# Layer norms finished on VectorE, X itself turned, the modulation row fetched ahead of them

## The chip, the core and the metric

The kernel runs on one core of a Trainium2 chip. The metric is device time in microseconds of one execution. The core has TensorE (matrix products and turnings, in the rows PE, its weight loads PEld), VectorE (DVE), ScalarE (ACT), GpSimd (POOL) and SyncE (SP), which issues most DMAs. Each engine runs its own list of instructions in order and waits on semaphores that others raise.

## The reference

256 rows of 1024 numbers pass through a post-norm block of two layers and then a block with modulation. Per layer of the first block:

```python
x = layer_norm(ALPHA * x + y, ln_g[i, 0], ln_b[i, 0])        # y: mLSTM mixer, or pooling mixer
x = layer_norm(ALPHA * x + memory_cross_attn(x, ...), ln_g[i, 1], ln_b[i, 1])
x = layer_norm(ALPHA * x + sq_relu_mlp(x, ...), ln_g[i, 2], ln_b[i, 2])
# layer_norm: (x - mean) * rsqrt(var + eps) * g + b
# sq_relu_mlp: square(relu(x @ w1 + b1)) @ w2 + b2
```

The second block takes six vectors from `c`: `silu(c) @ w_ada + b_ada` (the modulation row), normalizes by root mean square, scales and shifts by them, and runs a mixer of two kinds of attention and a SwiGLU; the reference's last step is a norm with `g_final`.

## The kernel before

All arithmetic is in float32 made of two parts: for every product the operand is split into a high part (type fp32r) and a low part (the rest), and three products are summed: high by high, low weight by high, high weight by low. ScalarE makes the high part of each 1 MB piece of weights (`hi_to`, L971), VectorE the low part (`lo_to`, L1504), in rings of four pieces (`raw`, `wh`, `wl`). SyncE refills a `raw` place as soon as its low part is made. So VectorE's list sets when pieces arrive.

`X` and `U` hold the 256 rows as two tiles of 128 (`t` = 0, 1) by 1024 columns, in halves `h` of 512. `XH`, `XL` hold the same turned, columns on partitions, high and low. A layer norm (`layer_norm`, `turn_norm`, `ln_head`) goes: VectorE adds the sublayer's output to ALPHA times X (L1718), takes statistics (L1721 to L1725); GpSimd makes the inverse root (L2133); VectorE writes z = (u - mean) * r into U (L1735); TensorE turns U (`ln_turn`, L413); ScalarE and VectorE apply g and b, now one number per partition, while they empty the bank (L1118, L1677), and make high and low parts (L1123, L1681, L1686). GpSimd makes X itself out of U later, row by row, with g and b copied to all partitions (`bv`; L2166, L2168), and before an MLP it multiplies X by ALPHA and adds the bias b2 (L2175, L2177). Two norms, at the end of each layer (`layer_norm_rows`), write X on VectorE (L1750, L1757).

`pair` is the first product behind a norm: two weight pieces by the rows of t = 0, then of t = 1, while VectorE is still busy with t = 1. In the cross-attention (`xattn`) four heads go through scores (L601), softmax, turning (L611), ScalarE's copy of the turned weights (`turned`, L1169), and the product with the values (L620). In the MLP (`mlp`), 16 steps j: `up(j)` (L329 to L336), ScalarE's relu (L1212), its square as high part (L1220), the same square in float32 on VectorE (L1817), the low part from it (L1821, tile `FLT`), and `down(j)` (L348 to L357). Twelve steps of each MLP also bring in 1 MB of `w_ada`, which VectorE adds into `MOD` (L1493). `MOD` starts as zeros (L2189) with b_ada in its first row (L2190, semaphore `d_mod`); both are on GpSimd's list, behind the first two norms of the first layer.

## Time and profile before

| | us |
|---|---|
| three timed runs | 1053.34 (median), 1053.26, 1059.33 |
| profiled execution, its own time | 1058.63 |
| its span, first to last instruction | 1056.8 |
| TensorE busy / its weight loads | 992.2 / 894.7 |
| VectorE / ScalarE / GpSimd busy | 711.5 / 494.1 / 148.8 |
| mean granted TensorE clock | 0.975 |

The profiled execution took 1.83 us more than its span. Its own time is 5.29 us over the median; of the timed runs two lie by 1053.3 and one by 1059.3.

### The profile page before, as it was taken

The numbers are of one execution on the slowest core, as the hardware profiler recorded it, in microseconds if no ns is written. First come the engines' busy times: TensorE is split into PE (matmuls) and PEld (weight loads), VectorE is DVE, ScalarE is ACT, GpSimd is POOL, SyncE is SP. The second block draws the span as 40 slices with busy tenths as digits, with TensorE's granted clock in tenths as the row PEclk, the third lists the DMA queues.
The fourth block names the chain that finished last, engine by engine and source line by source line (L and its number), as shares of the span: only waits on it lengthen the run. The fifth ranks groups of instructions, "written<-read, shape, count | busy, mean of one in ns | idle before, by whom it ended". The sixth has DMA issues, their size and how long they took to land.

```text
span 1056.8 us, 15072 instructions
## 1 busy us (share of the span) xinstructions
PE 992.2 (94%) x6249; PEld 894.7 (85%) x6249; DVE 711.5 (67%) x815; ACT 494.1 (47%) x674; POOL 148.8 (14%) x122
## 2 busy tenths in 40 slices
PE   6999999899399999989997999999999899999997
PEld 6877988888298998888886998997989689999996
DVE  4874568856687776798599867746786775544453
ACT  4665365436144444354363444443766574334341
POOL 0000111605700001125057000000400000000000
PEclk9999999999699999999998999999999999999999
DMA  8773362723588787627337987852654238565521
GB/s 281 249 239 120 120 223 96 239 87 113 181 309 283 260 292 243 206 80 239 94 114 244 339 296 256 299 157 84 188 178 145 95 104 267 167 200 167 192 80 40
DMA packets 114527, 200.03 MB, mean 189 GB/s; under 512 B 5122, under 2 KB 85368, under 8 KB 111388
## 3 DMA queue, kind: packets, MB, share of 16 engines
q1 hardware_dynamic: 111340, 188.38, 53.4%
q0 software_dynamic: 2832, 10.16, 2.7%
q8 instruction: 50, 0.82, 0.3%
q10 hardware_dynamic: 288, 0.52, 0.1%
q14 instruction: 17, 0.14, 0.0%
HBM read 198.00 MB, written 1.05 MB: 188 GB/s over the span
## 4 chain that ended last, share of the span: by engine, by line
PE 72%; DVE 14%; ACT 5%; issue 4%; POOL 3%; DMA 2%; SPq 1%; DVEq 0%; POOLq 0%; ACTq 0%
PE YB L357 11%; PE YB L348 11%; PE YB L353 10%; PE WB L329 10%; PE WB L336 10%; PE WB L332 10%; DVE wl L1504 6%; PE WB L353 2%; PE WB L348 2%; PE WB L357 2%; ACT wh L971 2%; PE WB L620 2%; DMA raw<-in_mlstm_w_in 1%; DVE BN L1721 1%; DVE U L1718 1%
## 5 line engine op out<-in xcount | busy, mean ns | idle before, releaser
L1504 DVE TENSOR_TENSOR wl<-raw,wh 128x2048 fp32r<-128x2048 f32 (+2 forms) x153 | 370.0, 2427 | 137.4 <-ACT wh L971 136.8
L971 ACT CAST wh<-raw 128x2048 fp32r<-128x2048 f32 (+2 forms) x153 | 288.9, 1892 | 58.9 <-PE YB L357 26.3
L329 PE MATMUL WB<-XH,wh 128*128 128x256 f32 x1024 | 146.7, 285 | 1.3 <-ACT XH L1044 1.3
L332 PE MATMUL WB<-XH,wl 128*128 128x256 f32 x1024 | 144.0, 283 | 0.0
L336 PE MATMUL WB<-XL,wh 128*128 128x256 f32 x1024 | 143.7, 283 | 0.0
L357 PE MATMUL YB<-wh,FLT 128*128 128x512 f32 x360 | 115.9, 404 | 26.3 <-DVE FLT L1821 26.3
L329 PEld LDWEIGHTS WB<-XH,wh 128*128 128x128 f32 x1024 | 135.3, 192 | 6.0 <-ACT AR L1022 1.7
L332 PEld LDWEIGHTS WB<-XH,wl 128*128 128x128 f32 x1024 | 132.4, 192 | 0.0
L336 PEld LDWEIGHTS WB<-XL,wh 128*128 128x128 f32 x1024 | 132.1, 192 | 0.0
L348 PE MATMUL YB<-wh,FHT 128*128 128x512 f32 x360 | 115.9, 404 | 0.0
L353 PE MATMUL YB<-wl,FHT 128*128 128x512 f32 x360 | 114.2, 399 | 0.0
L357 PEld LDWEIGHTS YB<-wh,FLT 128*128 128x128 f32 x360 | 69.2, 193 | 42.9 <-DVE FLT L1821 27.2
L353 PEld LDWEIGHTS YB<-wl,FHT 128*128 128x128 f32 x360 | 69.2, 192 | 16.7
L348 PE MATMUL YB<-wh,XH 128*128 128x256 f32 (+3 forms) x336 | 76.2, 339 | 4.0 <-ACT XH L1123 3.5
L348 PEld LDWEIGHTS YB<-wh,FHT 128*128 128x128 f32 x360 | 66.9, 194 | 12.9
L357 PE MATMUL YB<-wh,XL 128*128 128x256 f32 (+3 forms) x336 | 71.7, 330 | 1.0 <-DVE XL L1841 0.8
L353 PE MATMUL YB<-wl,XH 128*128 128x256 f32 (+3 forms) x336 | 72.0, 331 | 0.0
L1493 DVE SCALAR_TENSOR_TENSOR AR<-raw,SM,AR 128x2048 f32<-128x2048 f32 x24 | 58.6, 2441 | 15.9 <-DMA AR<-in_b_ada 15.2
L348 PEld LDWEIGHTS YB<-wh,XH 128*128 128x128 f32 x336 | 53.1, 192 | 10.5 <-ACT XH L1123 5.0
L357 PEld LDWEIGHTS YB<-wh,XL 128*128 128x128 f32 x336 | 52.9, 191 | 6.8 <-DVE XL L1841 1.0
L353 PEld LDWEIGHTS YB<-wl,XH 128*128 128x128 f32 x336 | 52.8, 191 | 5.2
L2133 POOL TENSOR_TENSOR BN<-BN,SM 128x1 f32<-128x1 f32 x18 | 10.7, 593 | 304.3 <-DVE BN L1725 303.8
(314 smaller groups left out, 1081.7 us busy)
## 6 DMA issues: line engine op xcount, KB each, us to landing
raw<-in_mlp_w SPq DMA_DIRECT2D x64, 1024.0 KB, 5.6
raw<-in_w_ada SPq DMA_DIRECT2D x24, 1024.0 KB, 5.7
raw<-in_mlstm_w_in SPq DMA_DIRECT2D x12, 1024.0 KB, 7.4
raw<-in_w_ffn_gate SPq DMA_DIRECT2D x11, 1024.0 KB, 5.3
raw<-in_w_ffn_up SPq DMA_DIRECT2D x11, 1024.0 KB, 5.4
raw<-in_w_ffn_down SPq DMA_DIRECT2D x11, 1024.0 KB, 4.9
raw<-in_mem_w_kv SPq DMA_DIRECT2D x8, 1024.0 KB, 5.4
raw<-in_xattn_wq SPq DMA_DIRECT2D x8, 1024.0 KB, 6.1
```

The source lines that it names most:

```text
L329: e.matmul(o, H[:, at(k)], xh[:, k, :], start=k == 0, stop=False)
L332: e.matmul(o, L[:, at(k)], xh[:, k, :], start=False, stop=False)
L336: f = e.matmul(o, H[:, at(k)], xl[:, k, :], start=False, stop=k == a - 1)
L348: e.matmul(o, xh[:, k0 + k, tk], pick(H, k), start=start and k == 0, stop=False)
L353: e.matmul(o, xh[:, k0 + k, tk], pick(L, k), start=False, stop=False)
L357: f = e.matmul(o, xl[:, k0 + k, tk], pick(H, k), start=False, stop=stop and k == a - 1)
L620: p = e.matmul(W[:, 256 * d:256 * d + 256], VM[:, m, 256 * h + 128 * d:256 * h + 128 * d + 128], PT[:, 256 * m:256 * m + 256], start=m == ...
L971: f = e.copy(w[:, 0:a * b], raw[:, 0:a * b])
L1493: e.scalar_tensor_tensor(acc, raw[:, :], CACT[:, k:k + 1], acc, ALU.mult, ALU.add).then_inc(w_ada.add(n))
L1504: f = e.tensor_tensor(L[:, 0:a * b], raw[:, 0:a * b], H[:, 0:a * b].bitcast(F32), ALU.subtract)
L1718: e.scalar_tensor_tensor(U[:, t, cs], X[:, t, cs], alpha, YB[2 * t + h][:, :], ALU.mult, ALU.add).then_inc(dve_ln.add(("u", s, t, h)))
L2133: e.tensor_tensor(o, x, MH[:, 0:o.shape[1]], ALU.pow).then_inc(sem_)
```

## The change

- Every layer norm is now one class, `Norm`. `head` is as before; `centre` writes (u - mean) * g into U, `scale` writes that times r plus b into X, both on VectorE and by halves. TensorE turns X, four blocks in one bank; ScalarE casts a half to XH with one copy, VectorE takes the low part from the bank (`low`). GpSimd no longer updates X. The norms of the second block keep U.
- b2 / ALPHA is added to X on VectorE in steps 4 to 7 of an MLP, and ALPHA stays in `head`.
- In the MLP ScalarE squares into float32 and then copies to the high part; VectorE's own square is gone.
- The zeros of MOD and the b_ada row come ahead of the first norm on GpSimd's list.
- In `pair`, low parts of weights by high parts of rows come before the high weights by low parts, and the turning of t = 1 is split in halves between the products. Behind the amid place of `rows` only half of t = 0 is turned there, the other half after the last product.
- In `xattn` ScalarE casts one more piece of weights ahead of the first softmax, and the first copy of turned weights comes ahead of the second softmax. In the mLSTM the first two heads come ahead of the first keys piece.
- In the norm behind the pooling mixer, low parts of the mixer come between the two halves of `head`, and one low part of weights ahead of the second tile.

```diff
+                def first(n, t):
+
+                    hi = ln_hi(s, t) if n == 0 else None
+                    e.wait_ge(*w_hi[ms[n]])
+                    part(n, t, WH, XH, range(4), hi, start=True)
+                    e.wait_ge(*w_lo[ms[n]])
+                    part(n, t, WL, XH, range(4))
+                    part(n, t, WH, XH, range(4, 8), hi)
+                    part(n, t, WL, XH, range(4, 8))
+
+                for n in range(2):
+                    e.wait_ge(*free(n))
+                    first(n, 0)
+                part(0, 0, WH, XL, range(8), ln_lo(s, 0), stop=True)
+                ln_turn(s, 1, 0)
+                part(1, 0, WH, XL, range(8), stop=True)
+                ln_turn(s, 1, 1)
+                for n in range(2):
+                    first(n, 1)
+                    key = ("pair",) + names[n]
+                    part(n, 1, WH, XL, range(8), ln_lo(s, 1) if n == 0 else None, stop=True).then_inc(cnt.add(key))
+                    ends[ms[n]] = cnt[key]
...
+            def by_row(s):
+
+                return s not in ("mix", "ffn")
+
+            def ln_turn(s, t, h):
+
+                if by_row(s):
+                    e.wait_ge(*dve_ln["x", s, t, h])
+                    turn(("ln", s, t, h), lambda k: X[:, t, 128 * k:128 * k + 128], range(4 * h, 4 * h + 4), pe_turn)
...
+                s = f"{i}{j}"
+                for t in range(2):
+                    for h in range(2):
+                        W = bank_of.get(("ln", s, t, h), WB[0])
+                        e.wait_ge(*pe_turn["ln", s, t, h])
+                        e.copy(XH[:, 4 * h:4 * h + 4, 128 * t:128 * t + 128],
+                               W[:, :].rearrange("p (k c) -> p k c", k=4)).then_inc(act_ln.add(("hi", s, t, h)))
+                    if t == 0:
+                        hi_to(m)
...
                 q(2)
+                hi_to(M["wq", i, 3] + 3)
                 scores(0)
                 q(3)
+                turned(0)
                 scores(1)
...
-                    W, R = bank_of.get(("w1", i, j), WB[0]), R0[:, 512 * (j % 2):512 * (j % 2) + 512]
+                    W, R = bank_of.get(("w1", i, j), WB[0]), R0[:, 0:512]
+                    RS = R0[:, 512 + 512 * (j % 2):1024 + 512 * (j % 2)]
...
+                        e.wait_ge(*dve_mlp["h", i, j - 2])
+                    e.activation(RS, R, ACT.Square).then_inc(act_mlp.add(("s", i, j)))
+                    if j > 1:
                         hi_to(M["w2", i, j - 2] + 3)
                         e.wait_ge(*ends.get(M["w2", i, j - 2], (act_own, 1)))
-                    e.activation(FH[j % 2], R, ACT.Square).then_inc(act_mlp.add(("h", i, j)))
+                    e.wait_ge(*act_mlp["s", i, j])
+                    e.copy(FH[j % 2], RS).then_inc(act_mlp.add(("h", i, j)))
...
+                def centre(self, t, h):
+                    s, cs = self.s, slice(512 * h, 512 * h + 512)
+                    e.wait_ge(*self.g_in)
+                    e.scalar_tensor_tensor(U[:, t, cs], U[:, t, cs], BN[:, t, 12:13], BV[self.g][:, cs],
+                                           ALU.subtract, ALU.mult).then_inc(dve_ln.add(("c", s, t, h)))
+
+                def scale(self, t, h):
+                    s, cs = self.s, slice(512 * h, 512 * h + 512)
+                    e.wait_ge(*self.b_in)
                     e.wait_ge(*po_ln["r", s, t])
-                    e.tensor_scalar(U[:, t, cs], U[:, t, cs], BN[:, t, 12:13], BN[:, t, 14:15], ALU.subtract, ALU.mult
-                                    ).then_inc(dve_ln.add(("z", s, t, h)))
-
...
+                    e.wait_ge(*dve_ln["c", s, t, h])
+                    e.scalar_tensor_tensor(X[:, t, cs], U[:, t, cs], BN[:, t, 14:15], BV[self.b][:, cs],
+                                           ALU.mult, ALU.add).then_inc(dve_ln.add(("x", s, t, h)))
+
+                def low(self, t, h):
+                    s = self.s
+                    W, at_ = bank_of.get(("ln", s, t, h), WB[0]), (slice(None), slice(4 * h, 4 * h + 4),
+                                                                  slice(128 * t, 128 * t + 128))
+                    e.wait_ge(*act_ln["hi", s, t, h])
+                    e.tensor_tensor(XL[at_], W[:, :].rearrange("p (k c) -> p k c", k=4), XH[at_].bitcast(F32),
+                                    ALU.subtract).then_inc(dve_ln.add(("lo", s, t, h)))
+                    freed["ln", s, t, h] = dve_ln["lo", s, t, h]
+
+                def first(self):
+
                     for h in range(2):
...
+                        self.centre(0, h)
+                        self.scale(0, h)
+
+                def second(self):
+
+                    self.head(1, 0)
+                    self.head(1, 1)
+                    self.centre(1, 0)
+                    self.low(0, 0)
+                    self.scale(1, 0)
+                    self.low(0, 1)
+                    self.centre(1, 1)
+                    self.scale(1, 1)
+                    self.low(1, 0)
+                    self.low(1, 1)
...
-                    step(e.tensor_tensor(RS, R, R, ALU.mult))
                     if j > 1:
                         lo_to(M["w2", i, j - 2] + 3)
+                    RS = R0[:, 512 + 512 * (j % 2):1024 + 512 * (j % 2)]
                     e.wait_ge(*act_mlp["h", i, j])
                     e.tensor_tensor(FL[j % 2], RS, FH[j % 2].bitcast(F32), ALU.subtract
                                     ).then_inc(dve_mlp.add(("h", i, j)))
+                    if 4 <= j < 8:
+                        n, b_in = bv_of.get(("b2", i), (0, (d_bv[0], 16)))
+                        t, h = divmod(j - 4, 2)
+                        cs = slice(512 * h, 512 * h + 512)
+                        e.wait_ge(*b_in)
+                        e.scalar_tensor_tensor(X[:, t, cs], BV[n][:, cs], 1 / ALPHA, X[:, t, cs], ALU.mult, ALU.add
+                                               ).then_inc(dve_mlp.add(("b2", i, t, h)))
...
+            n10 = Norm(1, 0, "pool", lambda t, h: dve_ln["x", "02", t, h])
+            n10.head(0, 0)
+            pool_lows(1)
+            n10.head(0, 1)
+            n10.first()
+            lo_to(M["pool",] + 2)
+            n10.second()
             lo_to(M["pool",] + 3)
...
-                e.wait_ge(*dve_ln["lo", s, 1, 3])
-                for t in range(2):
-                    e.wait_ge(*g_in)
-                    step(e.tensor_tensor(X[:, t, :], U[:, t, :], BV[gi][:, :], ALU.mult))
-                    e.wait_ge(*b_in)
-                    e.tensor_tensor(X[:, t, :], X[:, t, :], BV[bi][:, :], ALU.add).then_inc(po_x.add((s, t)))
-                users[:] = [po_x[s, 1]] * 2
+                users[:] = [dve_ln["x", s, 1, 1]] * 2
 
             def before_mlp(i):
-                n, b_in = bvec(("b2", i), I["mlp_b2"][i])
-                e.wait_ge(*po_x[f"{i}1", 1])
-                for t in range(2):
-                    step(e.tensor_scalar(X[:, t, :], X[:, t, :], ALPHA, None, ALU.mult))
-                    e.wait_ge(*b_in)
-                    e.tensor_tensor(X[:, t, :], X[:, t, :], BV[n][:, :], ALU.add).then_inc(po_x.add((f"mlp{i}", t)))
-                users[n] = po_x[f"mlp{i}", 1]
+                n, _ = bvec(("b2", i), I["mlp_b2"][i])
+                users[n] = dve_mlp["b2", i, 1, 1]
...
             e.wait_ge(*pe_mlstm["c", 3, 1])
+            step(e.memset(MOD, 0.0))
+            e.dma_start(MOD[0:1, :], I["b_ada_2"][0].rearrange("(a c) -> a c", a=1)).then_inc(d_mod, 16)
             layer_norm(0, 0)
             layer_norm(0, 1)
-            step(e.memset(MOD, 0.0))
-            e.dma_start(MOD[0:1, :], I["b_ada_2"][0].rearrange("(a c) -> a c", a=1)).then_inc(d_mod, 16)
             e.dma_start(WM, I["c_win"]).then_inc(d_wm, 16)
```

GpSimd's list from the second norm's X updates (before) and from the last mLSTM head (changed) on:

```order
L2166 TENSOR_TENSOR X<-U,bv 128x1024
L2168 TENSOR_TENSOR X<-X,bv 128x1024
L2189 MEMSET AR 128x6144
L2190 DMA AR<-in_b_ada 1x16x384
L2191 DMA AR<-in_c_win 128x1088
L2128 DMA bv<-in_mlp_b 128x1024
L2175 TENSOR_SCALAR X<-X 128x1024
```

```order
L2229 TENSOR_TENSOR SM<-SM 128x1
L2257 MEMSET AR 128x6144
L2258 DMA AR<-in_b_ada 1x16x384
L2209 DMA bv<-in_ln_g 128x1024
L2209 DMA bv<-in_ln_b 128x1024
L2214 TENSOR_TENSOR BN<-BN,SM 128x1 x2
```

The zeros and the b_ada row stood behind the X updates; now they stand ahead of the first norm's g and b, and no X update is left.

VectorE's list from the second tile of the norm ahead of the first MLP up to the MLP's first low part (L1821, now L1889):

```order
L1735 TENSOR_SCALAR U<-U,BN 128x512 x2
L1677 TENSOR_SCALAR S<-WB,PC 128x128 x2
L1681 CAST XH<-S 128x2x128
L1677 TENSOR_SCALAR S<-WB,PC 128x128 x2
L1681 CAST XH<-S 128x2x128
L1686 TENSOR_TENSOR XL<-S,XH 128x2x128 x4
L1504 TENSOR_TENSOR wl<-raw,wh 128x2048 x2
L1493 SCALAR_TENSOR_TENSOR AR<-raw,SM,AR 128x2048
L1504 TENSOR_TENSOR wl<-raw,wh 128x2048
L1817 TENSOR_TENSOR AR<-AR 128x512
L1821 TENSOR_TENSOR FLT<-AR,FHT 128x512
```

```order
L1790 SCALAR_TENSOR_TENSOR U<-U,BN,bv 128x512
L1806 TENSOR_TENSOR XL<-WB,XH 128x4x128
L1798 SCALAR_TENSOR_TENSOR X<-U,BN,bv 128x512
L1806 TENSOR_TENSOR XL<-WB,XH 128x4x128
L1790 SCALAR_TENSOR_TENSOR U<-U,BN,bv 128x512
L1798 SCALAR_TENSOR_TENSOR X<-U,BN,bv 128x512
L1806 TENSOR_TENSOR XL<-WB,XH 128x4x128 x2
L1559 TENSOR_TENSOR wl<-raw,wh 128x2048 x2
L1548 SCALAR_TENSOR_TENSOR AR<-raw,SM,AR 128x2048
L1559 TENSOR_TENSOR wl<-raw,wh 128x2048
L1889 TENSOR_TENSOR FLT<-AR,FHT 128x512
```

The copies out of the bank and VectorE's square went; centre, scale and low part alternate. Two pieces of weights, the w_ada piece (L1493, now L1548) and one more piece still stand ahead of the first low part of the MLP.

ScalarE's list in the cross-attention; L1159 (now L1210) is the exponential, L1169 (now L1220) the copy of turned weights:

```order
L971 CAST wh<-raw 128x2048
L1150 COPY AR<-WB 128x512 x2
L1159 ACTIVATE AR,SM<-WB,SM 128x256 x2
L971 CAST wh<-raw 128x2048
L1150 COPY AR<-WB 128x512
L1159 ACTIVATE AR,SM<-WB,SM 128x256 x2
L1169 COPY AR<-WB 128x512
```

```order
L1016 CAST wh<-raw 128x2048
L1201 COPY AR<-WB 128x512 x2
L1016 CAST wh<-raw 128x2048
L1210 ACTIVATE AR,SM<-WB,SM 128x256 x2
L1201 COPY AR<-WB 128x512
L1220 COPY AR<-WB 128x512
L1210 ACTIVATE AR,SM<-WB,SM 128x256 x4
```

The cast of weights went ahead of the first exponential, and the copy ahead of the second.

## Rows read from the trace of the kernel before

**Rows 1.** The page's first part: busy time of TensorE, share of the span.

```profile
PE 992.2 (94%) x6249; PEld 894.7 (85%) x6249; DVE 711.5 (67%) x815; ACT 494.1 (47%) x674; POOL 148.8 (14%) x122
```

**Rows 2.** TensorE's waits: line, who ended them; us in total, times, longest.

```profile
PE YB L357 <- DVE FLT L1821: 26.3, 2, 18.3
...
PE WB L620 <- ACT AR L1169: 5.3, 2, 2.7
...
PE YB L348 <- ACT XH L1123: 3.5, 6, 0.6
```

**Rows 3.** Busy time by stretch, with granted clock, DMA share and rate.

```profile
core 0: us, PE busy (x) PEld busy (x) DVE busy (x) ACT busy (x) POOL busy (x), PEclk, DMA share, GB/s
...
260.00:285.00 25.00, 6.68 (x36) 5.58 (x35) 11.68 (x6) 4.82 (x7) 22.86 (x11) 0.63 0.46 164
...
335.00:430.00 95.00, 95.00 (x614) 86.56 (x614) 67.17 (x41) 43.57 (x42) 6.27 (x4) 1.00 0.79 265
```

**Rows 4.** Timeline of TensorE, 263 to 288 us (start, length, instructions, idle before).

```profile
263.14 0.62 PE L353 MATMUL YB<-wl,FHT 128*128 128x512 f32 x2
...
282.08 1.22 PE L357 MATMUL YB<-wh,FLT 128*128 128x512 f32 x2 [18.32 <-DVE FLT L1821]
...
287.31 0.63 PE L357 MATMUL YB<-wh,FLT 128*128 128x512 f32 x2
```

**Rows 5.** Timeline of VectorE over the same stretch.

```profile
251.43 6.71 DVE L1504 TENSOR_TENSOR wl<-raw,wh 128x2048 fp32r<-128x2048 f32 x2
...
273.29 2.35 DVE L1493 SCALAR_TENSOR_TENSOR AR<-raw,SM,AR 128x2048 f32<-128x2048 f32 x1 [15.15 <-DMA AR<-in_b_ada]
...
280.62 1.41 DVE L1821 TENSOR_TENSOR FLT<-AR,FHT 128x512 fp32r<-128x512 f32 x1
```

**Rows 6.** Timeline of GpSimd over the same stretch.

```profile
251.59 4.39 POOL L2166 TENSOR_TENSOR X<-U,bv 128x1024 f32<-128x1024 f32 x1 [5.72 <-DVE XL L1686]
...
265.15 5.22 POOL L2189 MEMSET AR<- 128x6144 f32 x1
...
270.66 0.60 POOL L2190 DMA_DIRECT2D AR<-in_b_ada  x1 [0.29 <-POOL AR L2189]
```

**Rows 7.** Timeline of VectorE at the second MLP's start.

```profile
548.00 4.50 DVE L1493 SCALAR_TENSOR_TENSOR AR<-raw,SM,AR 128x2048 f32<-128x2048 f32 x1
```

**Rows 8.** Timeline of TensorE at the second MLP's start.

```profile
561.68 1.22 PE L357 MATMUL YB<-wh,FLT 128*128 128x512 f32 x2 [7.97 <-DVE FLT L1821]
...
566.97 0.69 PE L357 MATMUL YB<-wh,FLT 128*128 128x512 f32 x2
```

**Rows 9.** Timeline of VectorE in front of the first cross-attention.

```profile
182.62 15.51 DVE L1504 TENSOR_TENSOR wl<-raw,wh 128x2048 fp32r<-128x2048 f32 x4
```

**Rows 10.** Timeline of TensorE in the first cross-attention.

```profile
208.07 3.12 PE L620 MATMUL WB<-AR,KV 128*128 128x256 f32 x8 [2.67 <-ACT AR L1169]
...
213.72 1.89 PE L620 MATMUL WB<-AR,KV 128*128 128x256 f32 x8
...
215.80 0.71 PE L348 MATMUL YB<-wh,XH 128*128 128x512 f32 x2
```

**Rows 11.** VectorE groups by form (busy us, mean ns | idle before): z, shifted rows.

```profile
L1735 DVE TENSOR_SCALAR U<-U,BN 128x512 f32<-128x512 f32 x16 | 8.0, 544 | 2.4 <-POOL BN L2133 2.0
...
L1757 DVE SCALAR_TENSOR_TENSOR X<-U,BN,bv 128x512 f32<-128x512 f32 x8 | 5.7, 748 | 0.1
```

**Rows 12.** Timeline of TensorE, mLSTM output and third normalization turned.

```profile
150.83 0.62 PE L357 MATMUL YB<-wh,FLT 128*128 128x512 f32 x2
...
460.80 1.04 PE L413 MATMUL WB<-IDN,U 128*128 128x128 f32 x8
```

**Rows 13.** Timeline of VectorE at the same two places.

```profile
144.93 2.15 DVE L1658 SCALAR_TENSOR_TENSOR FLT<-WB,PC,FHT 128x128 fp32r<-128x128 f32 x8
...
465.78 2.29 DVE L1504 TENSOR_TENSOR wl<-raw,wh 128x2048 fp32r<-128x2048 f32 x1
```

**Rows 14.** DMA issues: KB each, median us from issue to landing.

```profile
bv<-in_ln_b POOLq DMA_DIRECT2D x6, 512.0 KB, 5.0
```

More of the change, by code:

```diff
@@ L387, in pair, with part @@
                 ms = [M[n] for n in names]
-                for t in range(2):
-                    for n, m in enumerate(ms):
-                        if t == 0:
-                            e.wait_ge(*free(n))
-                        f = tm(m, 8, 256, 0, 256, YB[n][:, 256 * t:256 * t + 256], t, 0, True, True,
-                               hi=ln_hi(s, t) if n == 0 else None, lo=ln_lo(s, t) if n == 0 else None,
-                               amid=(lambda: ln_turn(s, 1)) if t == 0 and n == 1 else None)
-                        if t == 1:
-                            f.then_inc(cnt.add(("pair",) + names[n]))
-                            ends[m] = cnt[("pair",) + names[n]]
+                def part(n, t, w, x, ks, wait=None, start=False, stop=False):
+                    for k in ks:
+                        if wait:
+                            wait(k)
+                        f = e.matmul(YB[n][:, 256 * t:256 * t + 256], x[:, k, 128 * t:128 * t + 128],
+                                     w[ms[n] % NS][:, 256 * k:256 * k + 256], start=start and k == 0,
+                                     stop=stop and k == 7)
+                    return f
+                def first(n, t):
[18 more added lines that the diff above has]
+                    ends[ms[n]] = cnt[key]
             def turn_pair(key, src, ready, cnt):
@@ L651, in xattn @@
                 values(3)
-                rows(s_, 2, [("wo", i, 2), ("wo", i, 3)], [x(2), x(3)], False, True, amid=lambda: ln_turn(after, 0))
+                rows(s_, 2, [("wo", i, 2), ("wo", i, 3)], [x(2), x(3)], False, True, amid=lambda: ln_turn(after, 0, 0))
+                ln_turn(after, 0, 1)
             def mlp(i, s, late=None):
@@ L1765, in xattn, with layer_norm @@
+            def layer_norm(i, j, rows, x_in):
+                n = Norm(i, j, rows, x_in)
+                n.head(0, 0)
+                n.head(0, 1)
+                n.first()
+                n.second()
             def xattn(i):
@@ L1877, in vector @@
             mlp(1, KV, late)
-            head, centre, scale = layer_norm_rows(1, "w21", lambda t: po_x["mlp1", t])
+            n12 = Norm(1, 2, "w21", lambda t, h: dve_mlp["b2", 1, t, h])
             def rms_z(s, t, h):
```

210 lines of the change are left out of this document (93 added, 117 removed).

## The prediction

> **What bounds the kernel now.** I read the page's busy times first: TensorE is at work in 94% of the span [rows 1], so only its remaining idle time and time at the lower clock can be won. In 95 us of an MLP in full flow all 95.00 are TensorE's, at clock 1.00 [rows 3]; an edit to another engine's work is worth nothing there unless it makes that engine late. So I went to the list of TensorE's waits. Three entries matter [rows 2]: the MLP's low part FLT (26.3 us in two waits), the turned softmax weights (5.3 in two), and the high parts behind the norms (3.5 in six). The timelines around these say why, and what else is lost beside the wait.
>
> At the first MLP's start TensorE has nothing from 263.76 to 282.08 [rows 4]. VectorE holds FLT back until 280.62, since ahead of it stands a w_ada piece that waited 15.15 us for b_ada's row in MOD [rows 5]. That row is fetched at 270.66, behind GpSimd's X updates of 4.39 us and up each and behind the zeros, which run from 265.15 for 5.22 us [rows 6]. In 260 to 285 us the granted clock is 0.63 [rows 3], and behind the idle time, from 282.08 to 287.31, the products still go at about half speed, the 1.2 GHz level [rows 4].
>
> At the second MLP's start b_ada has long been there, but the same w_ada piece takes 4.50 us [rows 7] where the first took 2.35 with GpSimd idle of SBUF work [rows 5], and TensorE waits 7.97 us [rows 8]. The pieces ahead of it are slow too: two low parts in 6.71 us [rows 5], four in 15.51 [rows 9], 3.4 to 3.9 each, against 2.29 for one alone [rows 13]. The slow ones lie beside X updates. I read it as the two engines getting in each other's way.
>
> **The change part by part.** All sums are made against the profiled execution's 1058.63 us; the median of the runs is 5.29 lower, and I take the gain off the median.
>
> *First MLP.* The b_ada fetch goes ahead of the first norm, some 100 us before its need. With X updates gone, VectorE's path from 251.43 is two low parts (2×2.29), w_ada (2.35), one low part (2.29) and FLT's 0.7: 9.9 us, so FLT at 261.3. TensorE needs it at 263.76, so the 18.32 goes whole, with 2.4 us in hand. What is late next is that same list; the norm in front of it must not grow by more than that. The clock should then not fall, and of 5.23 us at half speed 2.6 return. Together 20.9.
>
> *Second MLP.* Doubling gone, VectorE saves 2.15 on w_ada and over 2 on each low part ahead of it, more than the 7.97. The stall goes, and half of 561.68 to 566.97 [rows 8], 2.6: together 10.6. Its margin by the same list is 2.3.
>
> *Cross-attentions.* From 205.40 (208.07 less its wait) to 215.80 [rows 10] are 10.40 us. The work in it is twice eight value products with four turnings (213.72 to 215.80, 2.08) and eight scores, which I price like the eight products of 1.89: 6.05. So 4.35 are lost, 2.67 as the listed wait and the rest as slow progress around it. VectorE was late by the four low parts: 15.51 would be 9.2. ScalarE's copy ahead of the second softmax no longer stands behind exponentials that wait for VectorE. I leave 0.2: 4.15 each, 8.3 for both, the second attention taken to be like the first because its wait is [rows 2].
>
> *Norms.* Centre and scale are four instructions of 748 ns a tile, 3.0 us, where z took two of 544, 1.1 [rows 11]: 1.9 us more on VectorE's path per tile. It is hidden as long as `pair` has products of t = 0 to do while t = 1 is finished. In return four copies and casts a tile go, and TensorE no longer waits for a cast per block: of the 3.5 us in six waits I take 1.0 as won, since low parts, which now come later, may take their place. Bounds: 3.5 won, or 12 tiles × 1.9 = 23 lost.
>
> *Norm behind the pooling mixer.* This is the place where I expect a loss. TensorE turns the first tile at 460.80 [rows 12], with little queued behind. A low part of weights, 2.29, which stood at 465.78 behind the second tile's statistics [rows 13], now stands ahead of the whole second tile. X's low parts follow that. I price one such wait, 2.3, less 0.7 that earlier turning gives back: 1.6 lost. The g and b rows land 5.0 us after issue [rows 14], which is just in time; bounds 0 and 5.0 lost.
>
> *Zeros ahead of the first norm.* The 5.22 us now fall beside VectorE's eight low parts at 144.93, 2.15 us in all [rows 13], and weights behind them, which TensorE needs from 150.83 on [rows 12]. If they are doubled as at the X updates [rows 7], 150.83 is still met: 0. If VectorE is shut out for all 5.22, it is met 1.5 late. I take 0; the doubling of rows 7 is nearer to it than a full block.
>
> The Trainium skill, page SBUF — State Buffer, section Who interferes with whom, says that a VectorE instruction with two SBUF inputs contends with a GpSimd instruction that reads SBUF, and not with one that only writes it. The slowed subtractions beside X updates agree with the first half [rows 5, 7]. By its second half the zeros cost nothing, and the sum stays as it is.
>
> *MLP steps.* ScalarE gets one more copy a step and VectorE loses a square. ScalarE is busy 43.57 of 95 us [rows 3], in 614 products, 8.5 steps; a copy of under 0.8 us adds 7 us. Hidden; without that cover 32 × 0.8 = 26. The eight b2 additions, 0.75 each [rows 11], lie beside full TensorE: VectorE is busy 67.17 of 95 [rows 3]. Cost 0.
>
> *Order in the mLSTM, pair and mixer*: rearrangements with no wait of size behind them: +0.5, bounds −2 and +2.
>
> Sum: 20.9 + 10.6 + 8.3 + 1.0 − 1.6 + 0.5 = 39.7. That is 1018.9 for the profiled execution and 1013.6 off the median, so 1014. Likely 1006 to 1022.
>
> **The rivals.** *The longer norm shows.* If the 1.9 us a tile is exposed at every tile, 23 of the 39.7 are lost: 1037. At half of the tiles 1025. For it: turning now needs a scaled X, one more step behind the inverse root, and the margins at the MLPs are only 2.4. Against: behind most norms the products of t = 0 in `pair` last longer than a tile's finish, and present waits there are 0.6 at the longest [rows 2].
>
> *GpSimd is not what slows VectorE.* Then only the wait for b_ada goes. FLT would be done at 280.62 + 1.41 − 15.15 = 266.9 [rows 5], 3.1 us after TensorE's need; the second stall and the attention's stay. Gain 18.3 − 3.1 + 2.6 = 17.8: 1035 or 1036. Against: VectorE's slow low parts lie exactly beside X updates, and one alone takes 2.29.
>
> *It does not do what it says.* Another wait takes b_ada's place ahead of FLT, say raw pieces landing late while VectorE is early: TensorE stays idle, clock low, and the time is within 1%, 1047. In 260 to 285 DMA is at 0.46 [rows 3], so there is room, which speaks against.
>
> *Slower: the weights cannot keep up.* Each of 24 steps brings three pieces, 3.1 MB, in about 11.1 us, 280 GB/s; rows 3 have 265 at a DMA share of 0.79. The stalls let the rings fill; without them the transfers could set the pace. The point of decision is where 39.7 us are lost in 24 steps, 1.65 each: 12.8 us a step, 246 GB/s. At 200 it would be 15.7 a step, 110 us lost, 1124. Against it: TensorE went through 95 us at this rate without a gap [rows 3].
>
> **How the numbers follow.** Forecast 0.62; the longer norm showing 0.22 (1025 to 1037); GpSimd innocent 0.08 (1035); no effect 0.05; slower 0.03. The range of 1005 to 1029 holds the forecast and the smaller half of the second case, 0.8 together; its low end adds the upper bounds of the norms (2.5) and of the rearrangements, and part of the 1.83 us around the span. 1%, 10.5 us, is about what a measurement of this kernel can tell from no change. Faster by more 0.92, within it 0.05, slower by more 0.03.
>
> **What the changed profile would show.** If right: no wait of TensorE for FLT at either MLP's start, and granted clock 1.00 there; low parts of weights near 2.3 us everywhere; GpSimd's busy time at about half of its 148.8 [rows 1]; the attention's listed wait under 0.7; perhaps a new wait of 2 to 3 us for low parts behind the pooling norm. The longer norm would show as TensorE waits for X or XL of 1 to 4 us at most norms. If GpSimd is innocent, low parts of 3 to 4 us remain with no X update beside them. Slow weights would show as VectorE and ScalarE waiting for raw through the MLPs, with gaps in TensorE. I am wrong if the early zeros or the new order of norm steps hold up TensorE somewhere that is free of waits now.

## The result and the profile after

| | median us | runs | ratio to the kernel before |
|---|---|---|---|
| before | 1055.95 | 1053.26 to 1059.33, 4 | |
| changed | 1021.68 | 1021.55 to 1024.9, 4 | 0.9681 [0.964, 0.9723] |

The changed kernel is 34 us faster by the medians. Its profiled execution took 1024.9 us (span 1023.1), the profiled one of before 1058.63: 33.7 less. 39.7 were forecast.

The page's first part of the changed kernel:

```profile
PE 986.8 (96%) x6249; PEld 892.6 (87%) x6249; DVE 657.7 (64%) x759; ACT 496.2 (49%) x662; POOL 61.4 (6%) x98
```

TensorE is busy 96% of the span instead of 94% [rows 1], and GpSimd 61.4 us instead of 148.8. Of TensorE's list of waits, the wait for FLT, 26.3 us before [rows 2], is no longer in it, and that for the turned softmax weights neither. New are these two (line, who ended them; us in total, times, longest):

```profile
PE YB L393 <- DVE XL L1806: 3.6, 5, 2.0
...
PE WB L435 <- DVE X L1798: 3.1, 4, 2.4
```

Both traces hold the same 6249 products, in nearly the same order, so the start of the n-th in one can be subtracted from that in the other. The table has the places between which the difference moves (minus: the changed kernel is ahead); "step" is what the stretch gave (minus) or cost.

```
stretch (us in the trace of before)          difference behind it   step
start to 75                                          0.1             0.1
mLSTM, 75 to 114                                    -2.2            -2.3
mLSTM to the first norm, 114 to 199                 -2.6            -0.4
first cross-attention, 199 to 223                   -7.2            -4.5
norm ahead of the first MLP, 223 to 261             -7.2             0.0
start of the first MLP, 261 to 292                 -28.1           -20.9
first MLP, 292 to 443                              -28.1             0.0
pooling mixer and its norm, 443 to 481             -24.0            +4.1
second cross-attention, 481 to 520                 -28.5            -4.5
norm ahead of the second MLP, 520 to 551           -28.5             0.0
start of the second MLP, 551 to 577                -39.2           -10.7
second MLP, 577 to 716                             -39.2             0.0
modulation and its norm, 716 to 757                -35.9            +3.3
second block, 833 to 846                           -34.3            +1.6
norm ahead of the SwiGLU, 846 to 882               -33.8            +0.6
882 to the end                                     -33.8             0.0
```

At the first MLP VectorE's timeline answers rows 5 (start, length, instructions, idle before):

```profile
244.54 4.48 DVE L1559 TENSOR_TENSOR wl<-raw,wh 128x2048 fp32r<-128x2048 f32 x2
...
248.94 2.35 DVE L1548 SCALAR_TENSOR_TENSOR AR<-raw,SM,AR 128x2048 f32<-128x2048 f32 x1
...
253.40 0.69 DVE L1889 TENSOR_TENSOR FLT<-AR,FHT 128x512 fp32r<-128x512 f32 x1
```

Two low parts take 4.48 together instead of 6.71, the w_ada piece starts without a wait and takes 2.35, and FLT is there at 254.09. TensorE's timeline at the two MLPs, where rows 4 and rows 8 had the stalls:

```profile
256.42 0.64 PE L357 MATMUL YB<-wh,FLT 128*128 128x512 f32 x2
...
525.07 0.64 PE L357 MATMUL YB<-wh,FLT 128*128 128x512 f32 x2
```

Both first products with FLT start at full speed and without an idle time ahead of them. FLT is done 2.3 us before the first of them starts (254.09 and 256.42): that is its margin. VectorE at the second MLP, which answers rows 7:

```profile
517.67 2.34 DVE L1548 SCALAR_TENSOR_TENSOR AR<-raw,SM,AR 128x2048 f32<-128x2048 f32 x1
...
522.13 0.69 DVE L1889 TENSOR_TENSOR FLT<-KV,FHT 128x512 fp32r<-128x512 f32 x1
```

In the first cross-attention, which answers rows 10, the same eight value products follow each other without a wait:

```profile
202.60 1.89 PE L656 MATMUL WB<-AR,KV 128*128 128x256 f32 x8
...
206.50 1.97 PE L656 MATMUL WB<-AR,KV 128*128 128x256 f32 x8
...
208.66 0.71 PE L348 MATMUL YB<-wh,XH 128*128 128x512 f32 x2
```

The zeros of MOD now run beside VectorE's eight low parts of the mLSTM. GpSimd's and VectorE's timelines there:

```profile
141.93 5.26 POOL L2257 MEMSET AR<- 128x6144 f32 x1
```

```profile
142.43 2.15 DVE L1713 SCALAR_TENSOR_TENSOR FLT<-WB,PC,FHT 128x128 fp32r<-128x128 f32 x8
144.71 4.49 DVE L1559 TENSOR_TENSOR wl<-raw,wh 128x2048 fp32r<-128x2048 f32 x2
```

The eight low parts take 2.15 us as in rows 13. They read one operand from a bank (WB); the low parts of weights behind them read both from the memory, and the first of those, beside the zeros to its end, is no slower: 4.49 for two. 5.26 us of zeros cost VectorE nothing.

The loss of 4.1 lies at the norm behind the pooling mixer. TensorE's and VectorE's timelines there:

```profile
434.19 0.66 PE L435 MATMUL WB<-IDN,X 128*128 128x128 f32 x4 [2.36 <-DVE X L1798]
...
442.27 0.74 PE L393 MATMUL YB<-wh,XL 128*128 128x256 f32 x4 [2.05 <-DVE XL L1806]
...
443.53 0.94 PE L393 MATMUL YB<-wh,XL 128*128 128x256 f32 x4 [0.52 <-DVE XL L1806]
```

```profile
433.38 0.75 DVE L1798 SCALAR_TENSOR_TENSOR X<-U,BN,bv 128x512 f32<-128x512 f32 x1 [0.52 <-POOL BN L2214]
...
435.60 2.28 DVE L1559 TENSOR_TENSOR wl<-raw,wh 128x2048 fp32r<-128x2048 f32 x1
...
441.53 0.68 DVE L1806 TENSOR_TENSOR XL<-WB,XH 128x512 fp32r<-128x512 f32 x1
```

TensorE turned the first tile without a wait in rows 12. Now it waits 2.36 us for X and then, behind the products of `pair` that need only high parts, 2.05 and 0.52 for X's low parts: L1806 comes at 441.53, behind the low part of weights (435.60) and the second tile's statistics. In the table's stretch TensorE is idle for 6.5 us, where before it was idle for 3.5; the other 1.2 of the 4.1 are busy time, lengthened by a stretch at half clock (443.9, below). That part changes with the execution: in e9 and e10 below, which have the same instructions here, the half clock falls at 433.9 and 433.8, TensorE comes later to X's low parts, waits 0.9 for the first of them, and the step is 2.6 instead of 4.1.

The rest of the cost is clock. Busy time by stretch with the granted clock (the column behind POOL), first of the MLP's start that answers rows 3, then of the four stretches of the changed kernel, ahead of the last microseconds, that are at the lower level, 1.2 GHz:

```profile
core 0: us, PE busy (x) PEld busy (x) DVE busy (x) ACT busy (x) POOL busy (x), PEclk, DMA share, GB/s
...
250.00:275.00 25.00, 25.00 (x166) 22.89 (x165) 19.59 (x12) 16.87 (x21) 0.00 (x0) 1.00 0.99 364
...
443.90:447.30 3.40, 3.40 (x19) 3.40 (x18) 1.68 (x3) 0.59 (x1) 1.09 (x2) 0.50 0.19 42
...
679.40:686.20 6.80, 6.80 (x22) 5.80 (x22) 1.74 (x3) 0.00 (x0) 0.00 (x0) 0.50 0.37 109
...
703.30:710.10 6.80, 6.80 (x28) 6.80 (x28) 5.20 (x8) 3.62 (x6) 2.94 (x3) 0.50 0.30 76
...
802.30:805.70 3.40, 3.40 (x13) 2.92 (x12) 1.80 (x7) 2.64 (x10) 0.60 (x2) 0.50 0.02 5
```

The MLP's start is at 1.00 instead of 0.63, with DMA at a share of 0.99. Three stretches of 6.8, 6.8 and 3.4 us at 0.50 lie in the second block. In the trace of before two of 3.4 lie there, and one in each cross-attention:

```profile
208.70:212.10 3.40, 3.40 (x12) 2.77 (x11) 1.40 (x6) 1.62 (x6) 0.00 (x0) 0.50 0.45 158
...
498.90:502.30 3.40, 3.40 (x11) 2.74 (x11) 1.61 (x5) 2.09 (x6) 0.00 (x0) 0.50 0.38 135
...
720.70:724.10 3.40, 3.40 (x10) 2.62 (x9) 0.89 (x1) 0.00 (x0) 0.00 (x0) 0.50 0.39 89
...
741.20:744.60 3.40, 3.40 (x14) 3.40 (x14) 3.27 (x6) 3.18 (x6) 0.11 (x1) 0.50 0.00 0
```

At half speed a busy stretch costs up to half of its length: 8.5 us in the second block now, 3.4 then. The difference of 5.1 is about the 3.3 and the 1.6 of the table, though the change moves little there.

### The profile page after: what moved, and what is told of

It is laid out like the page before. It is cut to its first block, busy times and chain, and to the rows that moved or that the text cites. A ratio compares the mean times of both kernels' runs of the same rounds, so it can differ in the third digit from the quotient of the medians.

```text
span 1023.1 us, 14977 instructions
## 1 busy us (share of the span) xinstructions
PE 986.8 (96%) x6249; PEld 892.6 (87%) x6249; DVE 657.7 (64%) x759; ACT 496.2 (49%) x662; POOL 61.4 (6%) x98
## 4 chain that ended last, share of the span: by engine, by line
PE 82%; DVE 9%; ACT 4%; issue 2%; POOL 1%; SPq 1%; DMA 1%; DVEq 0%; POOLq 0%; ACTq 0%
PE WB L332 11%; PE WB L336 11%; PE WB L329 11%; PE YB L348 10%; PE YB L357 10%; PE YB L353 10%; PE YB L393 4%; PE WB L348 2%; PE WB L353 2%; PE WB L357 2%; ACT wh L1016 2%; DVE U L1777 2%; DVE wl L1559 2%; PE WB L656 1%; PE WB L637 1%
## 5 line engine op out<-in xcount | busy, mean ns | idle before, releaser
L1559 DVE TENSOR_TENSOR wl<-raw,wh 128x2048 fp32r<-128x2048 f32 (+2 forms) x153 | 347.7, 2280 | 191.3 <-ACT wh L1016 190.7
L357 PE MATMUL YB<-wh,FLT 128*128 128x512 f32 x360 | 113.6, 397 | 0.0
L1548 DVE SCALAR_TENSOR_TENSOR AR<-raw,SM,AR 128x2048 f32<-128x2048 f32 x24 | 56.3, 2345 | 0.0
L348 PE MATMUL YB<-wh,XH 128*128 128x512 f32 (+3 forms) x176 | 52.0, 389 | 0.4 <-ACT XH L1450 0.4
L357 PE MATMUL YB<-wh,XL 128*128 128x512 f32 (+3 forms) x176 | 49.8, 376 | 1.6 <-DVE XL L1916 1.4
L353 PE MATMUL YB<-wl,XH 128*128 128x512 f32 (+3 forms) x176 | 50.1, 379 | 0.0
L357 PEld LDWEIGHTS YB<-wh,XL 128*128 128x128 f32 x176 | 33.0, 196 | 7.4 <-DVE XL L1916 1.6
L353 PEld LDWEIGHTS YB<-wl,XH 128*128 128x128 f32 x176 | 33.1, 196 | 5.3
L348 PEld LDWEIGHTS YB<-wh,XH 128*128 128x128 f32 x176 | 32.2, 197 | 4.6 <-issue 0.6
L1180 ACT CAST XH<-WB 128x512 fp32r<-128x512 f32 x16 | 9.4, 587 | 54.9 <-PE WB L435 54.9
```

The costliest lines, as they stand in the source:

```text
L348: e.matmul(o, xh[:, k0 + k, tk], pick(H, k), start=start and k == 0, stop=False)
L353: e.matmul(o, xh[:, k0 + k, tk], pick(L, k), start=False, stop=False)
L357: f = e.matmul(o, xl[:, k0 + k, tk], pick(H, k), start=False, stop=stop and k == a - 1)
L1548: e.scalar_tensor_tensor(acc, raw[:, :], CACT[:, k:k + 1], acc, ALU.mult, ALU.add).then_inc(w_ada.add(n))
L1559: f = e.tensor_tensor(L[:, 0:a * b], raw[:, 0:a * b], H[:, 0:a * b].bitcast(F32), ALU.subtract)
```

## The experiments

Ratios are to the kernel before, run beside it on the same chip, with their 95% interval. What an execution's trace shows is compared product by product, as above; it is sharper than the medians, since the executions of one kernel spread by 2 to 9 us.

| run | edit | median us | ratio |
|---|---|---|---|
| e1_mod_alone | before + early zeros and row | 1047.13 | 0.9905 [0.9888, 0.9922] |
| e2_mod_late | changed − early zeros and row | 1020.56 | 0.9653 [0.9636, 0.9669] |
| e3_gpsimd_reads | changed + GpSimd reads | 1041.21 | 0.9852 [0.9833, 0.9872] |
| e4_gpsimd_writes | changed + GpSimd writes | 1025.07 | 0.9692 [0.9671, 0.9714] |
| e5_attn_order_back | changed − attention order | 1021.44 | 0.9676 [0.9633, 0.9718] |
| e12_attn_order_alone | before + attention order | 1050.18 | 0.9948 [0.993, 0.9966] |
| e6_pool_stats_first | pooling norm, first edit | 1021.54 | 0.9678 [0.9642, 0.9714] |
| e7_pool_lows_early | pooling norm, second edit | 1023.23 | 0.9683 [0.9639, 0.9728] |
| e8_pool_both | both | 1024.47 | 0.9696 [0.9657, 0.9734] |
| e9_square_back | changed − square on ScalarE | 1020.66 | 0.9661 [0.9634, 0.9688] |
| e10_mod_spread | small products spread | 1023.21 | 0.9692 [0.9673, 0.9712] |
| e11_spread_and_pool | e10 and e6 | 1026.05 | 0.971 [0.9685, 0.9734] |

**What made the stall at the first MLP.** Two causes stood ahead of FLT: the late row and the slowed pieces. Each was taken away alone.

e1, the kernel before with GpSimd's list changed:

```diff
+            step(e.memset(MOD, 0.0))
+            e.dma_start(MOD[0:1, :], I["b_ada_2"]...).then_inc(d_mod, 16)
             layer_norm(0, 0)
             layer_norm(0, 1)
-            step(e.memset(MOD, 0.0))
-            e.dma_start(MOD[0:1, :], I["b_ada_2"]...).then_inc(d_mod, 16)
```

> The kernel before with one edit: zeros of MOD and the b_ada row ahead of the first norm on GpSimd's list; the X updates stay there. Theory (two causes: the late b_ada row, and X updates that slow VectorE): the wait for b_ada goes, but the first w_ada piece and low parts stay at 3.4 to 4.5 us, so a stall of 3 to 8 us stays at the first MLP and 8 at the second, and the attentions' waits stay. 10 to 18 us under the kernel before: 1035 to 1043. Rival (the late row alone makes the stall): the whole 20.9 goes, 1032. Rival (GpSimd's backlog is the cause and the row's place is nothing): 1053.

VectorE's and then TensorE's timeline:

```profile
249.20 6.71 DVE L1504 TENSOR_TENSOR wl<-raw,wh 128x2048 fp32r<-128x2048 f32 x2
...
255.83 4.50 DVE L1493 SCALAR_TENSOR_TENSOR AR<-raw,SM,AR 128x2048 f32<-128x2048 f32 x1
```

```profile
268.24 1.22 PE L357 MATMUL YB<-wh,FLT 128*128 128x512 f32 x2 [6.69 <-DVE FLT L1821]
```

The wait for the row is gone, but beside the X updates two low parts still take 6.71 and the w_ada piece 4.50. 6.69 us of the 18.32 stay, inside the 3 to 8 expected, and some half clock. At this place the trace gained 11.4 of 20.9. The median fell by 9.7, a little under the expected gains, and 1047.13 lies outside the expected 1035 to 1043; the kernel before took 1056.86 beside it.

e2, the changed kernel with the opposite edit:

> The changed kernel with one part undone: zeros of MOD and the b_ada row behind the first two norms again. Theory (the row was late only because X updates stood ahead of it): with no X updates the row lands some 2 us before VectorE's first w_ada piece at 248.9 asks for it, no stall: 1021.6, within 2. Rival (the move of the row is what removed the stall): a stall of 10 us or more at the first MLP, 1032 to 1042.

GpSimd's and VectorE's timelines:

```profile
239.21 5.22 POOL L2259 MEMSET AR<- 128x6144 f32 x1
...
244.72 0.55 POOL L2260 DMA_DIRECT2D AR<-in_b_ada  x1 [0.29 <-POOL AR L2259]
```

```profile
248.99 2.35 DVE L1548 SCALAR_TENSOR_TENSOR AR<-raw,SM,AR 128x2048 f32<-128x2048 f32 x1
```

Without X updates on GpSimd's list the zeros start at 239.21, and the row, issued at 244.72, is there when VectorE asks at 248.99. There is no wait, and the time is that of the changed kernel. So the early place of the row, which took 11.4 us off the kernel before, gives nothing here: made first it gives 11.4 and leaves 9.5 to the rest of the change, made last it gives nothing. The rest of the change was enough for all 20.9.

**Whether GpSimd's reads slow VectorE.** e3 gives GpSimd its work back, on U, with results that nobody uses:

```diff
                 ln_stats(s)
+                e.wait_ge(*dve_ln["lo", s, 1, 1])
+                for t in range(2):
+                    e.wait_ge(*g_in)
+                    step(e.tensor_tensor(U[:, t, :], U[:, t, :], BV[gi][:, :], ALU.mult))
+                    e.wait_ge(*b_in)
+                    e.tensor_tensor(U[:, t, :], U[:, t, :], BV[bi][:, :], ALU.add)...
```

and the same with ALPHA and b2 ahead of each MLP. One wait, not shown above, holds the next norm's writing of U until GpSimd is done with it; e4 has the same one, and in the trace of e3 VectorE never stands at it.

> The changed kernel, and GpSimd again works at the places of the X updates: four operations of the same form and size behind each of the four norms, and four ahead of each MLP, on U, which nothing reads then (the results are thrown away). Theory (GpSimd's reads slow VectorE's two-operand instructions): low parts of 3.4 to 4.5 us return beside it, the attentions lose 2 to 4 each, both MLPs wait 6 to 8 for FLT and fall to half clock: 1040 to 1052. Rival (only the waits on the X updates' results mattered): 1021.6, within 2.

VectorE's timeline at the first MLP, and GpSimd's first operation there:

```profile
245.65 6.70 DVE L1559 TENSOR_TENSOR wl<-raw,wh 128x2048 fp32r<-128x2048 f32 x2
...
252.28 4.52 DVE L1548 SCALAR_TENSOR_TENSOR AR<-raw,SM,AR 128x2048 f32<-128x2048 f32 x1
```

```profile
245.82 4.38 POOL L2248 TENSOR_TENSOR U<-U,bv 128x1024 f32<-128x1024 f32 x1 [5.50 <-DVE XL L1808]
```

The old lengths are back (6.70 for two, 4.52 for the w_ada piece, as in rows 5 and 7), and TensorE waits 6.28 us for FLT at the first MLP and as long at the second. In the trace the first MLP's start lost 9.2, the second's 8.0, each attention 1.35, which is under the 2 to 4 expected. By the medians the time rose by 19.5; the two profiled executions differ by 14.5, since that of e3 has less half clock in the second block. The rival, that only the waits on X's new values mattered, falls.

e4 has in place of each of these operations five memsets of the same tile:

```diff
-                    step(e.tensor_tensor(U[:, t, :], U[:, t, :], BV[gi][:, :], ALU.mult))
+                    for _ in range(5):
+                        step(e.memset(U[:, t, :], 0.0))
```

> As the run with GpSimd reads, but each operation is five memsets of the same tile, which only write, for about the same busy time. Theory (an operation that reads is what gets in VectorE's way): low parts stay at 2.3 us, 1021.6 within 2. Rival (any GpSimd work on the memory slows VectorE): as with reads, 1040 to 1052.

```profile
244.48 5.01 POOL L2249 MEMSET U<- 128x1024 f32 x5 [5.49 <-DVE XL L1808]
```

```profile
244.33 4.49 DVE L1559 TENSOR_TENSOR wl<-raw,wh 128x2048 fp32r<-128x2048 f32 x2
...
248.73 2.35 DVE L1548 SCALAR_TENSOR_TENSOR AR<-raw,SM,AR 128x2048 f32<-128x2048 f32 x1
```

GpSimd is as busy, for 5.01 us beside the same two low parts, and they take 4.49, the w_ada piece 2.35. No wait returned in the trace; its execution took 1021.51 us. The median of 1025.07 is 1.5 above the expected bound; its interval overlaps that of the changed kernel, and no stall in the trace accounts for it. The three slower executions, 1024.75 to 1026.73, have granted clocks of 0.989, 0.987 and 0.987, those of the changed kernel at 1021.55 to 1021.76 have 0.992, 0.990 and 0.992; so the clock may be the reason, which is not shown.

The Trainium skill, page SBUF — State Buffer, section Who interferes with whom, states that VectorE's instructions with two inputs in the memory contend with GpSimd's reads, not with its writes. e3, e4 and the zeros at 141.93 agree with it. What the runs show of slowing is for GpSimd's operations with two inputs above all: beside one with one input, L2175 in the kernel before (272.40 to 275.20), the w_ada piece took its 2.35 us, while the short FLT beside another, at 280.62, took 1.41 instead of 0.69. Such operations were not tried alone.

**What made the waits of the cross-attentions.** e5 puts ScalarE's order back in the changed kernel:

```diff
-                hi_to(M["wq", i, 3] + 3)
                 scores(0)
                 q(3)
-                turned(0)
                 scores(1)
+                turned(0)
```

> The changed kernel with ScalarE's order in both cross-attentions as before: the fourth cast of weights behind the first softmax, the first copy of turned weights behind the second. Theory (slow low parts were the main cause there): the copy comes at 202.5 instead of 201.2 and ends 0.5 us after TensorE wants it, 0.5 lost in each attention, 1021.6 + 1, inside the spread of the runs; the trace shows the wait. Rival (the order is the main cause): 3 to 4 lost in each, 1028 to 1030. Rival (order is worth nothing): no wait at all.

```profile
205.36 1.97 PE L656 MATMUL WB<-AR,KV 128*128 128x256 f32 x8 [0.44 <-ACT AR L1220]
```

0.44 us of waiting in the first attention and as much in the second, 0.6 lost in each by the trace. e12 has the opposite edit in the kernel before:

> The kernel before with one edit: ScalarE's new order in both cross-attentions. The low parts there stay slow. Theory (with slow low parts the order matters, with quick ones hardly): with GpSimd's reads and the new order an attention lost 1.35 us where the kernel before lost over 4, so 2 to 3 come back in each, half of it as wait, the rest as half clock: 1049 to 1052 where the kernel before has 1056. Rival (the slow low parts alone make the wait): no gain.

In TensorE's list of waits the entry for the turned weights shrank from 5.3 in two:

```profile
PE WB L620 <- ACT AR L1169: 0.9, 2, 0.5
```

By the trace each attention gained 3.5. So the order alone gives 3.5 of 4.5, and the rest of the change without it, with its quick low parts, 3.9 of 4.5 (e5): again two edits that remove the same wait.

**The norm behind the pooling mixer.** e6 puts both halves of `head` ahead of the mixer's low parts, e7 puts the first tile's low parts of X ahead of the second tile's statistics, e8 does both; its edit is shown.

```diff
             n10.head(0, 0)
-            pool_lows(1)
             n10.head(0, 1)
+            pool_lows(1)
             n10.first()
             lo_to(M["pool",] + 2)
-            n10.second()
+            n10.low(0, 0)
+            n10.low(0, 1)
+            n10.head(1, 0)
+            n10.head(1, 1)
+            ...
```

> The changed kernel, in the norm behind the pooling mixer: both halves of the first tile's head ahead of the mixer's four low parts, as before the change. Theory (the 2.4 us wait for X comes from statistics that stand behind the low parts, so that GpSimd's root is late): the wait shrinks by about 0.9, 1020.7. Rival (the scaling itself makes it): no gain, or up to 1 lost since the mixer's last products now wait for low parts.

> The changed kernel, in the same norm: X's two low parts of the first tile ahead of the second tile's statistics, behind the low part of weights. Theory (the wait of 2 us for X's low parts comes from their place behind the whole second tile): that wait goes, and about 1.7 us of waiting for the second tile's X comes in its place, 0.9 gained, more if TensorE doesn't fall to half clock there; 1019 to 1021. Rival (casts or the low part of weights set it): no change.

> Both edits of that norm together. Theory: about 1.8 us less waiting than in the changed kernel, 1018 to 1020. Rival: one cancels the other, 1021.6.

VectorE's and TensorE's timelines of e6:

```profile
433.20 0.75 DVE L1798 SCALAR_TENSOR_TENSOR X<-U,BN,bv 128x512 f32<-128x512 f32 x1 [0.81 <-DMA bv<-in_ln_b]
```

```profile
430.79 0.51 PE L357 MATMUL YB<-wh,XL 128*128 128x256 f32 x2 [0.64 <-DVE XL L1916]
...
434.00 0.66 PE L435 MATMUL WB<-IDN,X 128*128 128x128 f32 x4 [1.28 <-DVE X L1798]
...
442.09 0.75 PE L393 MATMUL YB<-wh,XL 128*128 128x256 f32 x4 [2.04 <-DVE XL L1806]
```

The root is in time, but now b's row is not: 0.81 us of waiting for its transfer. The wait for X fell from 2.36 to 1.28; ahead of it stands a new one of 0.64 for the mixer's low parts, and the later 2.04 stays. The table's stretch became 0.2 us shorter than in the changed kernel. In e7 the wait for X's low parts went and this came in its place:

```profile
445.60 0.96 PE L435 MATMUL WB<-IDN,X 128*128 128x128 f32 x4 [1.80 <-DVE X L1798]
```

The stretch became 0.1 us longer, and with both edits 0.3 shorter. The chain from the mixer's output through two tiles of statistics, scaling and low parts is longer than the products that stand beside it, and moving its links only moves the wait. No edit of this kind gained what was expected.

**The square.** e9 puts VectorE's square back and lets ScalarE square into the high part, as before.

> The changed kernel with one part of the MLP undone: ScalarE's square goes straight to the high part again, and VectorE makes the same square in float32. Theory (both engines have room in the MLP): VectorE's first low part comes 0.7 us later, inside the 2.3 us in hand, 1021.6 within 1. Rival (VectorE's square was part of the stalls): a wait for FLT of 1 us or more at an MLP's start, 1024 or more.

```profile
253.18 0.69 DVE L1886 TENSOR_TENSOR AR<-AR 128x512 f32<-128x512 f32 x1
...
253.90 0.69 DVE L1890 TENSOR_TENSOR FLT<-AR,FHT 128x512 fp32r<-128x512 f32 x1
```

FLT comes 0.5 us later than in the changed kernel, inside its margin; no wait for FLT appears, and the time stays. The executions ran from 1016.38 us at a mean granted clock of 0.997 to 1024.67 at 0.989: 0.8% in both.

**Half clock in the second block.** TensorE's timeline of the changed kernel where one of its slow stretches begins:

```profile
676.97 4.59 PE L768 MATMUL WB<-AR 128*128 128x2 f32 x32
...
681.42 1.20 PE L348 MATMUL YB<-wh,FHT 128*128 128x512 f32 x2
```

32 instructions of two columns take 4.59 us, and the clock is at 0.50 from 679.4 on. e10 puts the 16 products of that row (two instructions each) one by one between the products of the MLP that follow it:

```diff
-                modulation(0, bank("mod"))
+                fill.extend([lambda k=k: piece(k) for k in range(16)])
 # in tm, behind each product of the high rows
+                    if fill:
+                        fill.pop(0)()
```

> The changed kernel with one edit on TensorE, at the end of the second MLP: the 16 products of the modulation that have two columns each stand one by one between the last products of the MLP, not in a row ahead of them. Theory (TensorE falls to half clock behind that row of small products): the half-clock stretch from 679 us on goes, up to 3.4 us come back, and the products themselves get no cheaper; 1018 to 1021. Rival (the fall has nothing to do with the row): the stretch stays and the time too, 1021.6.

> The changed kernel with two edits: the spread products of the modulation, and both halves of the first tile's statistics ahead of the mixer's low parts in the norm behind the pooling mixer. Theory: the gains add, 1017 to 1020, the fastest of all. Rival: at half-clock stretches that come and go the two can't be told from the changed kernel, 1020 to 1023.

Busy time from 675 to 725 us, with the granted clock, of e10 and of e11:

```profile
675.00:725.00 50.00, 47.12 (x273) 42.34 (x272) 33.42 (x54) 25.39 (x47) 13.42 (x16) 0.93 0.42 128
```

```profile
675.00:725.00 50.00, 47.12 (x232) 41.38 (x231) 27.51 (x51) 18.91 (x39) 7.11 (x11) 0.83 0.34 107
```

In the changed kernel this stretch has a clock of 0.86 on average. The fall at 679 is gone in e10, but TensorE then waits 1.1 and 1.7 us for VectorE's rows, and the clock falls at 700.0, in the second row of small products (697.31 to 701.65), for 6.8 us; in e11 it falls at 696.5, ahead of that row, for 17.1. Neither is faster: e10's 1023.21 lies above both values that were expected, e11's 1026.05 above both ranges, and the trace of e11 loses 3.6 us here. And in e5, which is the changed kernel here word for word, there was no fall at all:

```profile
675.00:725.00 50.00, 48.50 (x287) 42.57 (x286) 33.97 (x55) 27.16 (x51) 11.75 (x16) 1.00 0.45 144
```

So the row of small products isn't enough to bring the fall about, nor is its spreading enough to prevent it. When it comes in an execution stays open.

No version among these beats the changed kernel by more than the runs can tell; e2, e5, e6 and e9 are its equals.

## Why the prediction was right

1014 us were predicted, 1005 to 1029 as the range; 1021.68 came. Its two main causes, the late row and GpSimd's slowing of VectorE, are shown by e1, e3 and e4. By its steps:

- First MLP, 20.9: measured 20.9. Margin forecast at 2.4, measured 2.3. The prediction tied the 18.32 to the early fetch of the row together with the shorter path; e2 shows that the early fetch is not needed for it, and e1 that it alone gives 11.4.
- Second MLP, 10.6: measured 10.7. By e3 GpSimd's reads make 8.0 of it. The other 2.7 have no run of their own; in the kernel before VectorE's square (L1817), 2.82 us beside GpSimd's operations, also stood ahead of FLT.
- Cross-attentions, 8.3: measured 9.0. Of the 4.35 lost in each, what was put down as slow progress around the wait was a stretch at half clock, from 208.7 to 212.1, and in the second attention from 498.9 to 502.3. Of the two reasons given, VectorE's slow low parts and ScalarE's order, either one removed gives most of it (e5, e12).
- Zeros ahead of the first norm, 0: measured 0, by writes that don't disturb (141.93).
- MLP steps, 0: measured 0 through both MLPs, and e9.
- Norms, +1.0: −0.4, 0.0 and 0.0 in the table, so 0.4 won. The rival of the longer norm falls for the norms ahead of MLPs and attentions: 1.9 us more per tile are hidden there. Its bound of 12 tiles was too wide: the norms at the layers' ends had centre and scale on VectorE before [rows 11], so 8 tiles and 15 us were at stake.
- Norm behind the pooling mixer, −1.6: measured −4.1. The step is the term that was mis-sized. The place and the wait for low parts were right (2.05 and 0.52), but the wait for X, 2.36, wasn't in the sum, which even counted on an earlier turning, and busy time grew by 1.2 with a stretch at half clock. With the half clock elsewhere, in e9 and e10, the loss is 2.6. The rival of the longer norm came true at this one norm.
- mLSTM and rearrangements, +0.5: measured 2.3, of which 1.6 are a half-clock stretch at 79.0 that only the trace of before has.
- Not in the sum: the second block, −5.5. Of that 4.9 is half clock that differs from execution to execution, as e5 without any shows. The other 0.6 lies at the norm ahead of the SwiGLU (856 to 867) and is there in e2, e3, e4, e5 and e9 as well, so it comes with the change; its cause stays open.

Of the 6 us between 39.7 and 33.7 the pooling norm's 2.5 more and the second block's 5.5 are the loss, and 1.9 more than forecast came from the mLSTM (1.7), the attentions (0.7) and the second MLP (0.1), less 0.6 at the norms: 39.7 − 8.0 + 1.9 = 33.6. How near the sum comes is in part luck, since the clock differs by execution: against the same trace of before, the traces of e2 and e9, whose edits cost nothing, end 36.8 and 40.3 us earlier, that of the changed kernel 33.8. The rival in which GpSimd is innocent falls with e3. The one of slow weights falls with the DMA share of 0.99 at 250 to 275, 364 GB/s, without a gap in TensorE.

Two readings of the prediction were off without harm to its sum. The first w_ada piece's 2.35 us were not taken beside an idle GpSimd: L2175 ran beside it (272.40 to 275.20). And the slow low parts don't take 3.4 to 3.9 us each, which are means of merged rows; they take 2.29 or about 4.5, as the last section shows.

## What to carry to other kernels

Before an operation is moved to a free engine, look at what its neighbours' instructions take while it runs: here GpSimd, 14% busy, made VectorE's two-operand instructions last up to twice as long, and that showed as waits on a third engine. Two edits that remove the same wait don't add; undo each in the changed kernel and make each alone in the old one before giving either the credit. When waits are short, look for the half clock behind them as well as for the idle time: in the kernel before, 1.7 us of it stood behind a wait of 2.67 in the first attention, and 2.6 behind one of 7.97 at the second MLP.

## What the runs showed of the hardware that was not expected

Executions of one kernel differ by what the granted clock does. In the second block, from 675 us on, TensorE has the same instructions in the changed kernel, in e2, in e9 and in e5; at 0.50 were 17.0, 10.2, 6.8 and 0 us of it ahead of the last microseconds, in stretches of 3.4 or 6.8. From the changed kernel to e5 that gives back 6.7 us in the traces, as much as a 0.7% change of the kernel; it is not the whole half of 17.0, since without the falls TensorE waits longer for VectorE (U: 1.5 us in e5 instead of 0.8). So differences below 1% were read here from the traces, product by product, and not from medians of four to six runs.

GpSimd's reads cost VectorE more than was expected from GpSimd's small share of busy time: beside a stream of operations of 4.4 us a low part of 2.29 us took up to 4.51, while five memsets in 5.01 us cost it nothing. The two take turns. In the kernel before, of the two low parts in 6.71 us [rows 5], the one at 251.43 began ahead of GpSimd's operation (251.59) and took 2.29; the next began while GpSimd's ran and took 4.51. GpSimd loses as much: its operations beside low parts take 4.39 and 4.34, and the same two take 2.41 and 2.36 where VectorE waits for b_ada's row:

```profile
260.36 2.41 POOL L2166 TENSOR_TENSOR X<-U,bv 128x1024 f32<-128x1024 f32 x1
262.85 2.36 POOL L2168 TENSOR_TENSOR X<-X,bv 128x1024 f32<-128x1024 f32 x1
```

So some 2 of GpSimd's 4.4 us look like waiting for VectorE, as 2.2 of VectorE's 4.51 look like waiting for GpSimd.
